# Sample attention of a hybrid decoder step: cached keys turned by VectorE in 32x32 blocks, four pages to a tile, and the delta rule's steps set between key tiles

## The chip, the cores and the metric

The kernel runs on one core of a Trainium2 chip. The metric is the device time of one launch in microseconds; three runs of the kernel before gave 927.4, 928.0 and 933.94 us, so its median is 928.0. The profiled execution took 927.22 us, of which 925.6 lie between its first and last instruction (its span).

## What is computed

One step of a small hybrid decoder for 256 prompt tokens and for 8 sequences of 4 new tokens (288 token columns in all), in fp32: a SwiGLU layer, a mixing layer and a second SwiGLU layer, each with adaptive norms. The change lies in the mixing layer, whose two head groups work on the same projection:

```python
go, s_new = gated_delta_rule(gq, gk, gv, g_log, beta, s0)
mo = attend(mq, mk, mv)
out = jnp.concatenate([go, mo], axis=-1) @ w_out

def moba_sample(q, k, v, cache_k, cache_v, page_table):
    k_full = cache_k[page_table[:, : j * ppb]].reshape(b, j, MOBA_BLOCK, h, hd)
    kmean = jnp.mean(k_full.astype(jnp.float32), axis=2)
    gate = jnp.einsum("bqhd,bnhd->bqhn", q.astype(jnp.float32), kmean)
    _, idx = lax.top_k(gate, n_sel)
    l_sel = selected_logits(q, k_sel, t, idx, slopes)
    return attend_merged(l_sel, v_sel, l_own, v_own)
```

The delta rule has 4 heads of width 128 (9 problems of 128 tokens here), the attention 8 heads of 64. Each of the 8 sequences has 2048 past keys in 8 blocks, of which every row selects 3. The logits are q . k less a penalty in proportion to the distance, and the softmax joins the selected blocks with the own new keys. The prompt attends to its own 256 tokens only. Since any block may be selected by some row, the kernel reads all 128 key pages and all 128 value pages of the cache (128 keys x 512 numbers, 256 KB each, 67 MB together).

## The kernel before

**The order of the whole.** Everything before the mixing layer's attention (up to about 400 us) and everything from the output projection `w_out` on (664 us) is the same code in both kernels, but for small pieces. Each engine has one instruction stream, written out by hand; semaphores tie them. What is told below is the stretch between, from 402 to 664 us.

**The key phase (402 to 530 us).** The 8 sequences go in two groups of four (`g`), and each group through 8 blocks of 256 keys (`blk`): 16 steps `n`. A step loads eight pages (one block of four sequences), on two queues: SP's takes the even pages and POOL's the odd ones (`page`, L533 and L534: a page number is read into a register, then 256 KB are issued). Keys land with the key index on the partitions, but q . k needs the head dimension there. So for each of the four 128-wide chunks `c` of a step (`m` = 4n + c) PE transposes eight 128x128 tiles into two PSUM banks (`T`, L704), ACT copies one bank to `ktb` (L1465), DVE the other (L1855), and PE multiplies with the queries `Qbd`, four sequences side by side in 32-column strips of the array (`logits`, L1015). `block_logits` on DVE (L1795 to L1798) adds up each block for its gate, adds the distance penalty and takes the maximum. Between, at chunk 2 of steps 0 to 9, stand the prompt's attention (`attention` on PE, `normalise` and `biased` on DVE, two exponentials and a copy on ACT, one head a step) and, in steps 9 to 12, the sums of squares for the delta rule's q and k.

**The value phase (530 to 664 us).** The delta rule of the first head group is a chain of small steps on 9 problems of 128x128 (groups `g` of 4, 4 and 1): decay rows, transposed k and v, Gram products, then 7 levels `l` that build the inverse of a triangular matrix. A level is: `level_mask`, products `P` (L1187), a copy with scale on DVE (L1971), products `XP` and `PX` (L1196, L1200), and four to six subtractions on DVE (L1985, L1986). The products rotate over five PSUM banks, and `s_ge` counts the copies out. Between these steps stand 16 steps `values(n)`: PE transposes a block's probabilities (ACT's exponentials, L1278), DVE copies them (L1847), and PE multiplies with 8 value pages (L1055). V pages have room for four half-steps in `kv`. `selection(g)` picks blocks for 128 rows once a group is complete. At 540.8 us ACT issues the four loads of the delta states (L1515). SP loads `w_out` into `kv` as the last value steps free it, before the delta rule is through.

**The end.** DVE sets `s_gdn` when the delta rule's output is in `mix`; PE then starts the 128 products with `w_out` (L1251).

Of the kernel before, what the change touches and what calls it, by code (L numbers as in the profile page):

```python
# [51 lines left out]
KU = 12  # L52
PHASE = NB * NBLK
# [6 lines left out]
def const_layout():  # L60

    names = [("ident", P), ("ones", P), ("tri", P), ("later", P), ("triS", P), ("laterS", P),
             ("lev", 7 * P), ("mh8", P), ("lower8", 64), ("biasS", PAST), ("biasO", 64),
             ("dist", 3 * P), ("hmask", 512), ("selbt", 16), ("bdm", NB)]
    at, out = 0, {}
    for n, w in names:
        out[n] = (at, at + w)
        at += w
    return out, at


def make_consts():
# [20 lines left out]
    put("mh8", (i[:, None] % 4 == i[None, :] // NS) & (i[:, None] < 8))  # L93
    n, m = np.arange(64) // 8, np.arange(64) % 8
    put("lower8", np.broadcast_to(m < n, (P, 64)))
    h, t = (i % 32) // NT, i % NT
    slope = 2.0 ** -(h + 1.0)
    put("biasS", slope[:, None] * (np.arange(PAST)[None, :] - PAST - t[:, None]))
    own = np.zeros((P, 2, 32))
    for g in range(2):  # L100
        j = np.arange(32)
        ok = (j[None, :] // NT == 4 * g + i[:, None] // 32) & (j[None, :] % NT <= t[:, None])
        own[:, g, :] = np.where(ok, slope[:, None] * (j[None, :] % NT - t[:, None]), NEG)
    put("biasO", own.reshape(P, -1))
# [4 lines left out]
    put("hmask", h[:, None] == np.arange(512)[None, :] // HD)  # L109
    put("selbt", (i[:, None] // 32) * NT + t[:, None] == np.arange(16)[None, :])  # L110
# [4 lines left out]
def build_program(nc, a, o):  # L115
    lay, cwidth = const_layout()
    with ExitStack() as ctx:
# [57 lines left out]
        eps = sb("eps", [P, 1])  # L175
# [14 lines left out]
        ptab = sb("ptab", [1, 2 * PHASE], I32)  # L190
# [33 lines left out]
        gE = shaped(sgf, 2, P)  # L224
# [16 lines left out]
        RS = shaped(region[:, mq_at:mq_at + 8 * TOK], 8, TOK)  # L241
# [10 lines left out]
        dead = const[:, lay["biasS"][0]:lay["biasS"][1]]  # L252
        st = [shaped(region[:, mq_at + NB * P * x:mq_at + NB * P * (x + 1)], NB, P) for x in range(3)]
        st.append(shaped(dead[:, NB * P:2 * NB * P], NB, P))
# [12 lines left out]
        at_ = carver(region)  # L267
        S = at_(2, PAST)
        ktb = shaped(wflat[:, 8964:8964 + 2048], 2, 2, 512)
        extra = wring[:, 3]  # L270
        pT = shaped(dead[:, 0:512], 2, 2, P)
        Om = dead[:, 512:1024]
        pex = shaped(sgf, 2, BLK)
        Qbd = shaped(adaf, 4, NB, 32)
        gts = at_(2, NBLK)
        bmx = at_(2, NBLK + 1)
        pen = at_(2, NBLK + 1)
        cmpA = at_(64)
        cmpB = at_(64)
        cnt = at_(NBLK)  # L280
        negm = at_(2)
        sown = at_(2, 32)
        pown = at_(2, 32)
        rsum = at_(2, NBLK + 1)
        rin = at_(8)
        ownT = at_(2, P)
# [81 lines left out]
        s_ge = sem("s_delta_copied")  # L368
# [20 lines left out]
        s_bmx = sem("s_block_max")  # L389
        s_qz = sem("s_qbd_zero")  # L390
        s_qbd = sem("s_qbd_ready")
        s_kv = [[sem(f"s_kv{i}_page{y}_landed") for i in range(KU)] for y in range(2)]
        s_vq = [[sem(f"s_vquad{i}_half{y}_landed") for i in range(4)] for y in range(2)]
# [4 lines left out]
        s_kt = sem("s_kt_psum")  # L398
        s_ktA = sem("s_kt_copied_act")
        s_ktD = sem("s_kt_copied_dve")  # L400
        s_qk = sem("s_logits_psum")
        s_lev = sem("s_logits_copied")
        s_pen = sem("s_selection")
        s_po = sem("s_own_probs")
        s_pe = sem("s_sel_probs")
        s_PT = sem("s_sel_probsT_psum")
        s_oT = sem("s_own_probsT_psum")
        s_pTs = sem("s_sel_probsT_copied")
# [82 lines left out]
        def v_quad(q):  # L491
            return (q + 2) % 4
# [1560 lines left out]
```

## Time and profile before

| | us |
|---|---|
| median of three runs | 928.0 |
| profiled execution | 927.22 |
| its span | 925.6 |
| PE busy (share of the span) | 859.5 (93%) |
| DVE busy | 501.3 (54%) |
| ACT busy | 304.6 (33%) |
| POOL busy | 113.9 (12%) |
| 16 DMA queues' engines: mean rate over the span | 221 GB/s |

All times are read from one profiled execution, in microseconds from the start of its span. "Busy" counts the time in which an engine works on a recorded instruction. An fp32 matmul appears as two records, so "x8" in a row of PE stands for four products. An instruction's duration includes its start-up, and the next one on the same engine begins some 0.1 us before it is over; where operations follow each other, the difference of their starts is the cost. The clock column gives the granted clock of TensorE, 1.00 for 2.4 GHz and 0.50 for 1.2 GHz.

### The profile page before, as it was taken

Reading aid. Unit: us, or ns where it says so; the run is one execution under the profiler, and the core shown is the slowest. Engines: PE = TensorE matmul, PEld = TensorE weight load, DVE = VectorE, ACT = ScalarE, POOL = GpSimd, SP = SyncE. Lnnn points to the kernel's source line nnn. Section 1 sums busy time; section 2 is a strip of 40 time slices with the busy share of each in tenths; the row PEclk is TensorE's granted clock in tenths of the full one; section 3 lists DMA queues with packets and bytes.
Section 4 is the critical chain, followed back from the end, with each engine's and each line's share of the span. In section 5 each row is a group of like instructions: output and inputs, shape, how many; then the busy total and the mean of one; then the engine's idle time right before and its main releaser. Section 6 shows DMA issues by size and latency. Waiting matters only on the chain.

```text
span 925.6 us, 19660 instructions
## 1 busy us (share of the span) xinstructions
PE 859.5 (93%) x7464; PEld 751.7 (81%) x7464; DVE 501.3 (54%) x961; ACT 304.6 (33%) x499; POOL 113.9 (12%) x197
## 2 busy tenths in 40 slices
PE   4889999999999999999999848998899999999996
PEld 3789999998997999966656524665777999999996
DVE  1445454543355667566656566657446565544363
ACT  1333333332323336453434511000225334432331
POOL 2000000000021000132223223230130000000021
PEclk9999999999999999999999988999999999999999
DMA  9999979785755252378778698898391555434401
GB/s 323 370 307 357 308 255 312 253 320 185 300 199 182 92 182 59 125 243 268 230 232 289 205 369 289 296 333 311 87 338 57 167 182 176 145 137 156 159 1 51
DMA packets 122163, 204.83 MB, mean 221 GB/s; under 512 B 7548, under 2 KB 56982, under 8 KB 121970
## 3 DMA queue, kind: packets, MB, share of 16 engines
q1 hardware_dynamic: 104976, 163.08, 50.9%
q0 software_dynamic: 11648, 38.45, 12.4%
q10 hardware_dynamic: 5474, 2.39, 1.0%
q8 instruction: 46, 0.75, 0.3%
q14 instruction: 19, 0.16, 0.1%
HBM read 199.01 MB, written 4.88 MB: 220 GB/s over the span
## 4 chain that ended last, share of the span: by engine, by line
PE 83%; DVE 5%; DMA 4%; issue 2%; ACTq 2%; ACT 2%; POOL 1%; POOLq 1%; DVEq 0%; SPq 0%
PE bank L741 19%; PE bank L743 18%; PE bank L742 18%; PE bank L704 8%; PE bank L1015 3%; PE bank L1251 3%; PE bank L723 3%; PE bank L1055 2%; DMA kv<-in_cache_v 2%; ACTq L1515 2%; DMA wring<-in_w_ada 1%; DMA region<-in_x_sample 1%; DVE wring_rounded L1590 1%; PE bank L1200 1%; PE bank L1187 1%
## 5 line engine op out<-in xcount | busy, mean ns | idle before, releaser
L741 PE MATMUL bank<-hn_rounded,kv_rounded 128*128 128x288 f32 x928 | 276.7, 298 | 5.9 <-DVE wring_rounded L1590 4.1
L742 PE MATMUL bank<-xs_rounded,kv_rounded 128*128 128x288 f32 x928 | 274.4, 296 | 0.0
L743 PE MATMUL bank<-hn_rounded,wring_rounded 128*128 128x288 f32 x928 | 273.6, 295 | 0.0
L1590 DVE TENSOR_TENSOR wring_rounded<-wring,kv_rounded 128x1024 fp32r<-128x1024 f32 (+1 forms) x164 | 188.3, 1198 | 71.7 <-ACT kv_rounded L1311 71.6
L1311 ACT CAST kv_rounded<-wring 128x1024 fp32r<-128x1024 f32 (+1 forms) x164 | 158.5, 1026 | 162.0 <-PE bank L743 109.7
L741 PEld LDWEIGHTS bank<-hn_rounded,kv_rounded 128*128 128x128 f32 x928 | 174.4, 188 | 10.2 <-DVE wring_rounded L1590 4.7
L743 PEld LDWEIGHTS bank<-hn_rounded,wring_rounded 128*128 128x128 f32 x928 | 175.4, 189 | 0.0
L742 PEld LDWEIGHTS bank<-xs_rounded,kv_rounded 128*128 128x128 f32 x928 | 174.9, 189 | 0.0
L741 PE MATMUL bank<-region_rounded,kv_rounded 128*128 128x288 f32 x352 | 105.5, 300 | 1.6 <-DVE modT L1582 1.6
L742 PE MATMUL bank<-region_rounded,kv_rounded 128*128 128x288 f32 x352 | 104.6, 297 | 0.0
L743 PE MATMUL bank<-region_rounded,wring_rounded 128*128 128x288 f32 x352 | 104.2, 296 | 0.0
L1644 DVE TENSOR_TENSOR sgate<-sgate,bank 128x288 f32<-128x288 f32 x44 | 20.0, 454 | 131.1 <-PE bank L743 123.2
L741 PEld LDWEIGHTS bank<-region_rounded,kv_rounded 128*128 128x128 f32 x352 | 66.6, 189 | 2.4 <-DVE modT L1582 2.0
L743 PEld LDWEIGHTS bank<-region_rounded,wring_rounded 128*128 128x128 f32 x352 | 67.0, 190 | 0.0
L742 PEld LDWEIGHTS bank<-region_rounded,kv_rounded 128*128 128x128 f32 x352 | 66.8, 190 | 0.0
L1855 DVE COPY wring<-bank 128x512 f32<-128x512 f32 x64 | 44.1, 689 | 41.7 <-PE bank L704 40.7
L1465 ACT COPY wring<-bank 128x512 f32<-128x512 f32 x64 | 37.3, 584 | 70.4 <-PE bank L704 70.4
L1278 ACT ACTIVATE sgate<-bank 128x288 f32<-128x288 f32 x44 | 18.1, 412 | 104.5 <-PE bank L743 104.5
L704 PEld LDWEIGHTS bank<-const,kv 128*128 128x128 f32 x352 | 37.7, 141 | 17.3 <-ACT wring L1465 12.4
L704 PE MATMUL bank<-const,kv 128*128 128x128 f32 x352 | 47.9, 279 | 0.0
L641 POOL TENSOR_TENSOR xs<-h 128x288 f32<-128x288 f32 x21 | 14.0, 668 | 255.3 <-DVE h L1668 254.9
L534 POOL DMA_DIRECT2D kv<-in_cache_v x64 | 34.4, 537 | 84.5 <-issue 54.0
(275 smaller groups left out, 987.4 us busy)
## 6 DMA issues: line engine op xcount, KB each, us to landing
wring<-in_ffn_up SPq DMA_DIRECT2D x44, 1024.0 KB, 7.7
wring<-in_w_ada SPq DMA_DIRECT2D x36, 1024.0 KB, 10.9
wring<-in_ffn_down SPq DMA_DIRECT2D x16, 1024.0 KB, 7.3
kv<-in_cache_v SPq DMA_DIRECT2D x64, 256.0 KB, 4.9
kv<-in_cache_v POOLq DMA_DIRECT2D x64, 256.0 KB, 5.2
wring<-in_w_in SPq DMA_DIRECT2D x14, 1024.0 KB, 6.4
kv<-in_cache_k SPq DMA_DIRECT2D x44, 256.0 KB, 4.5
kv<-in_cache_k POOLq DMA_DIRECT2D x44, 256.0 KB, 4.8
```

The lines of the kernel that those rows point to most:

```text
L534: eng.dma_start(dst, cache[which][bass.ds(p, 1), :, :].rearrange("a p n -> (a p) n")).then_inc(landed, 16)
L704: return nc.tensor.transpose(out, in_, ident[0:n, 0:n])
L723: m = nc.tensor.matmul(out[32 * g:32 * g + 32, 0:P], cT[:, k, :], wring[:, slot, k, g * P:(g + 1) * P], start=(k == 0), stop=(k == KD - 1) ...
L741: nc.tensor.matmul(out, hi, rhs_hi, start=start, stop=False)
L742: nc.tensor.matmul(out, hi, rhs_lo, start=False, stop=False)
L743: return nc.tensor.matmul(out, lo, rhs_hi, start=False, stop=stop)
L1015: ins = mm(ps[4][32 * b4:32 * b4 + 32, 0:BLK], Qbd[:, c, 4 * (n // NBLK) + b4, :], ktb[:, c % 2, b4 // 2, (b4 % 2) * BLK:(b4 % 2 + 1) * BL ...
L1251: m = mm(ps[4 * (1 - g) + i][:, 0:TOK], wo[g][:, k, i * P:(i + 1) * P], mix[:, k, :], start=(k == 4), stop=(k == 3))
L1311: nc.scalar.copy(whiR[:, u % 2, c, :], wring[:, n % RING, c, :]).then_inc(s_whi, 1)
L1465: nc.scalar.copy(ktb[:, m % 2, 0, :], ps[2 * (m % 2)][:, :]).then_inc(s_ktA, 1)
L1590: v.tensor_tensor(wringR[:, slot, c, :], wring[:, slot, c, :], whiR[:, u % 2, c, :], ALU.subtract).then_inc(s_wlo, 1)
L1855: v.tensor_copy(ktb[:, m % 2, 1, :], ps[2 * (m % 2) + 1][:, :]).then_inc(s_ktD, 1)
```

## The change

**Key tiles.** A unit is now a quad: four consecutive pages of one sequence, 1 MB in one tile of 128x2048 (`quad(n)`, 32 for the keys and 32 for the values, `NQ` = 4 per sequence). DVE turns the keys in place, `v.transpose` on 32x32 blocks (`keys_turned`). After it partition 32i + d holds number d of a 32-number slice for keys 32i to 32i + 31. The queries are spread to match (`query_weights` on POOL, from 16 small products on PE), and PE forms the logits straight from the turned quad, 16 products of 128 columns (L1104 after). The 512 PE transposes, and the copies L1855 and L1465, are gone.

**Rows.** A row of the logits is now (head, key quarter, token) of one sequence, with 512 columns. ACT copies the logits out in 8 pieces of 64 columns with their sums (`logits_out`), POOL adds the penalty, DVE takes the maxima (`block_max`), and the selection works on four sequences at once, with gates and sums added over key quarters by one product each (`gates`, `sums`). The exponentials are 9 instructions a sequence (`exponentials`). Probabilities reach the layout for the values by 64 products of 32 columns each per sequence with a 0/1 matrix (`transposed`, L1135 after).

**Loads.** SP alone issues the pages; POOL's queue issues none. Eight quads are loaded ahead during the input projection, then a quad is issued once the fourth before it has been used (`consumed(n - 4)`), so four are in flight at most. `w_out` goes to `wring`, which the delta rule uses, and is issued after the last value quad and `s_gdn`.

**Order.** A list of 85 portions (`K` a key quad, `G` a selection, `X` exponentials, `T` a turn of probabilities, `R` sums, `V` a value quad, `O` the last result) is cut to 34 points by `turns`. Points 0 to 9 lie in the prompt's attention and hold key quads 0 to 15; points 10 to 32 lie in the delta rule and hold 53 portions, to value quad 18; point 33 holds the other 16, after the delta rule.

**Other engines.** ACT takes over from DVE 19 of the delta rule's copies (`BY_ACT`; counters `s_geA` and `s_geD`), POOL takes the level masks, the decay masks, `QD` and the spread of `VN`. The first tile of the second SwiGLU no longer waits for `w_out` to leave `kv`.

The core of the diff:

```diff
-        def page(eng, table, dst, which, landed):
-            p = eng.value_load(ptab[0:1, bass.ds(table, 1)], min_val=0, max_val=NPHYS - 1)
-            eng.dma_start(dst, cache[which][bass.ds(p, 1), :, :].rearrange("a p n -> (a p) n")).then_inc(landed, 16)
+            for n in range(2 * QUADS):
+                if n < 8 and n % 2 == 0:
+                    sp.wait_ge(*released(("in", (3, 4, 5, 6)[n // 2])))
+                elif n >= 8:
+                    sp.wait_ge(*consumed(n - 4))
+                load_quad(n)
+            sp.wait_ge(s_gdn, 1)
+            for g in range(2):
+                for k in range(2):
+                    sp.dma_start(wo[g][:, 4 * k:4 * k + 4, :], wout[:, 4 * k:4 * k + 4, 512 * g:512 * g + 512]).then_inc(s_wo[g], 16)
...
+        def turns(point):
+            def upto(i):
+                return (0, 2, 4, 5, 7, 8, 10, 11, 13, 14, 16)[i] if i <= 10 else 16 + (len(PORTIONS) - 32) * (i - 10) // 23
...
+            def logits(b, q):
+                n = NQ * b + q
+                pe.wait_ge(s_X, n + 1)
...
+                for j in range(4):
+                    for c in range(4):
+                        m = mm(ps[5 + 2 * (b % 2)][32 * c:32 * c + 32, P * q:P * q + P], W[b % 2][:, j // 2, 2 * c + j % 2, :],
+                               keys[:, :, 4 * c + j, :], start=(j == 0), stop=(j == 3), tile_position=(0, 32 * c))
...
+                for x in range(4 * NQ):
+                    for kb in range(4):
+                        m = mm(ps[5][32 * kb:32 * kb + 32, 32 * x:32 * x + 32], row[:, 32 * x:32 * x + 32], cst("pick")[:, 32 * kb:32 * kb + 32],
+                               start=True, stop=True, tile_position=(0, 32 * kb))
...
+            def keys_turned(n):
+                dve.wait_ge(*quad_landed(n))
+                v.transpose(quad(n), quad(n)).then_inc(s_X, 1)
...
-            for m in range(4 * 2 * NBLK):
-                dve.wait_ge(s_kt, 2 * m + 2)
-                dve.wait_ge(s_qk, m + 1)
-                v.tensor_copy(ktb[:, m % 2, 1, :], ps[2 * (m % 2) + 1][:, :]).then_inc(s_ktD, 1)
+            for s in range(HM + 2):
+                normalise(s)
+                biased(s)
...
+                attend(s)
```

**Where it moves instructions.** First DVE at level 1 of the delta rule. Before, between the two blocks of operations stand a mask pass and a copy of probabilities:

```order
L1971 TENSOR_TENSOR wring<-bank,region 128x512 x2
L1971 TENSOR_TENSOR wring<-bank,region 128x128
L1933 TENSOR_TENSOR wring<-wring,const 128x512 x2
L1843 COPY region<-bank 32x128
L1847 COPY const<-bank 128x256
L1985 TENSOR_TENSOR wring<-wring,bank 128x512
L1986 TENSOR_TENSOR wring<-wring,bank 128x512
```

The same place in the changed kernel (L2093 is the scaled copy, L2104 and L2105 are the subtractions, L1943 a turn of a key quad):

```order
L1943 STREAM_TRANSPOSE kv<-kv 128x2048
L1948 TENSOR_REDUCE region<-region 128x8
L1943 STREAM_TRANSPOSE kv<-kv 128x2048
L2093 TENSOR_TENSOR wring<-bank,region 128x512 x2
L2093 TENSOR_TENSOR wring<-bank,region 128x128
L1980 TENSOR_REDUCE cst<-bank 128x4
L1981 RECIPROCAL cst<-cst 128x4
L1983 TENSOR_TENSOR cT<-bank,const 32x128
L1943 STREAM_TRANSPOSE kv<-kv 128x2048
L2104 TENSOR_TENSOR wring<-wring,bank 128x512
L2105 TENSOR_TENSOR wring<-wring,bank 128x512
```

One to three key turns now stand in front of every step of the chain on DVE. On PE, in the program of before, the same level has the value products between `P` and `XP`:

```order
L1187 MATMUL bank<-wring 128x128 x9
L704 MATMUL bank<-const,region 32x128
L704 MATMUL bank<-const,sgate 128x128 x2
L1055 MATMUL bank<-kv,const 32x512 x8
L1061 MATMUL bank<-region 32x512 x4
L1196 MATMUL bank<-wring 128x128 x4
L1200 MATMUL bank<-wring 128x128 x4
```

In the changed kernel's program of PE (L1288 is `P`, L780 and L1123 are the own probabilities and the sums, L1104 the logits of a turned quad, L1296 and L1300 are `XP` and `PX`):

```order
L1288 MATMUL bank<-wring 128x128 x9
L780 MATMUL bank<-const,cst 32x128
L1123 MATMUL bank<-cst,const 128x36
L1104 MATMUL bank<-kv,adasb 32x128 x16
L1296 MATMUL bank<-wring 128x128 x4
L1300 MATMUL bank<-wring 128x128 x4
```

PE comes to `XP` only behind logits that wait for DVE's turns. From point 20 on value quads (16 products of 8 x 128 each) stand there, and at eight points the 64 small products of `transposed`.

## Rows read from the trace of the kernel before

**Rows 1.** Page, section 4: shares of the chain by line
```profile
PE bank L741 19%; PE bank L743 18%; PE bank L742 18%; PE bank L704 8%; PE bank L1015 3%; PE bank L1251 3%; PE bank L723 3%; PE bank L1055 2%; DMA kv<-in_cache_v 2%; ACTq L1515 2%; DMA wring<-in_w_ada 1%; DMA region<-in_x_sample 1%; DVE wring_rounded L1590 1%; PE bank L1200 1%; PE bank L1187 1%
```
**Rows 2.** By windows: busy us (xinstructions) per engine, clock, DMA share, GB/s
```profile
402.00:530.00 128.00, 123.04 (x1127) 77.78 (x1125) 82.66 (x186) 58.26 (x127) 31.20 (x58) 1.00 0.73 240
530.00:664.00 134.00, 108.38 (x924) 72.16 (x923) 83.54 (x199) 13.19 (x35) 33.10 (x61) 0.94 0.81 282
664.00:696.00 32.00, 31.28 (x128) 24.24 (x128) 14.22 (x29) 8.78 (x8) 12.36 (x16) 1.00 1.04 321
```
**Rows 3.** By windows: line L704 alone (transposes on PE)
```profile
402.00:530.00 128.00, 73.21 (x530) 56.41 (x528) 1.00 0.73 240
```
**Rows 4.** Groups by form, 400 to 664 us (count, busy us, mean ns)
```profile
L1855 DVE COPY wring<-bank 128x512 f32<-128x512 f32 x64 | 44.1, 689 | 41.7 <-PE bank L704 40.7
...
L1465 ACT COPY wring<-bank 128x512 f32<-128x512 f32 x64 | 37.3, 584 | 70.4 <-PE bank L704 70.4
```
**Rows 5.** Timeline of PE (start us, us, what): own logits, a key step
```profile
399.35 1.49 PE L972 MATMUL bank<-region,adasb 128*32 128x32 f32 x64 [1.90 <-DVE wring L1759]
...
446.88 0.64 PE L1015 MATMUL bank<-wring,adasb 128*32 128x256 f32 x8
447.45 1.09 PE L704 MATMUL bank<-const,kv 128*128 128x128 f32 x8
```
**Rows 6.** Timeline of DVE: one step of the prompt's attention
```profile
405.24 0.56 DVE L1780 SCALAR_TENSOR_TENSOR wring<-const,bank 128x384 f32<-128x384 f32 x1 [0.16 <-PE bank L984]
...
406.04 0.41 DVE L1784 TENSOR_REDUCE wring<-wring 128x1 f32<-128x256 f32 x1
...
410.94 0.29 DVE L1771 TENSOR_SCALAR wring<-wring 128x128 f32<-128x128 f32 x1
411.14 0.34 DVE L1772 TENSOR_SCALAR wring<-wring 128x256 f32<-128x256 f32 x1
```
**Rows 7.** Timeline of DVE: wide operations in SBUF
```profile
527.34 1.34 DVE L1873 COPY wring<-region 128x1152 f32<-128x1152 f32 x1
...
547.20 1.22 DVE L1919 TENSOR_TENSOR wring<-wring,const 128x1024 f32<-128x1024 f32 x1
```
**Rows 8.** Timeline of ACT and its queue: states issued, a probability
```profile
540.82 11.50 ACTq L1515 DMA_DIRECT2D region<-in_state_gdn  x3
552.36 3.44 ACTq L1515 DMA_DIRECT2D const<-in_state_gdn  x1
...
557.34 0.51 ACT L1278 ACTIVATE sgate<-region 128x256 f32<-128x256 f32 x1 [0.35 <-PE bank L704]
```
**Rows 9.** Timeline of PE: values and products of one level
```profile
611.19 1.92 PE L1055 MATMUL bank<-kv,const 128*32 128x512 f32 x16
613.04 1.16 PE L1196 MATMUL bank<-wring 128*128 128x128 f32 x8
614.04 1.06 PE L1200 MATMUL bank<-wring 128*128 128x128 f32 x8
```
**Rows 10.** Chain in order of time (start us, us, what)
```profile
605.43 3.63 PE bank L1161 x128
...
664.48 31.29 PE bank L1251 x128
```
**Rows 11.** By windows: after a wait of PE, and the value stream
```profile
576.00:578.00 2.00, 1.11 (x8) 0.19 (x8) 0.08 (x1) 0.00 (x0) 0.78 (x2) 0.82 1.00 393
578.00:580.00 2.00, 2.00 (x11) 1.60 (x8) 0.00 (x0) 0.00 (x0) 0.83 (x2) 0.50 1.04 402
...
630.00:640.00 10.00, 10.00 (x79) 5.74 (x72) 8.12 (x25) 0.00 (x0) 0.00 (x0) 1.00 1.03 371
```
**Rows 12.** Timeline of SP's queue: value pages issued in pairs
```profile
521.05 1.43 SPq L534 DMA_DIRECT2D kv<-in_cache_v  x2
...
523.25 1.42 SPq L534 DMA_DIRECT2D kv<-in_cache_v  x2
```
**Rows 13.** Groups by form of POOL over the span
```profile
L644 POOL TENSOR_TENSOR xs<-xs 128x288 f32<-128x288 f32 x18 | 15.3, 853 | 1.4
```

More of the change, by code:

```diff
@@ L552, in stream_rest @@
[L552 to L567 removed]
+        AB_TURN = 20
@@ L662, in _ @@
+            for point in range(29, POINTS + 1):
+                attend(point)
             pool.wait_ge(*copied(("S2",)))
@@ new lines, in attend @@
+            def attend(point):
+                for what, b, *q in turns(point):
+                    if what == "K":
+                        logits(b, q[0])
+                    elif what == "G":
+                        gates(b)
+                    elif what == "R":
+                        sums(b)
+                    elif what == "T":
+                        transposed(b)
+                    elif what == "V":
+                        values(b, q[0])
+                    elif what == "O":
+                        gathered(b)
@@ L1095, in bank @@
+            for s in range(HM + 2):
+                attention(s)
+                if s < 8:
+                    qk_sum(s)
+                attend(s)
             def bank(step):
@@ L1432, in _ @@
                 zqkv(q)
+            act.wait_ge(s_q4, 1)
+            nc.scalar.copy(sgf[:, 0:512], ps[6][:, :]).then_inc(s_q4e, 1)
             for q in range(0, 6, 2):
@@ new lines, in probs_transposed, with attend @@
+            def probs_transposed(b):
+                act.wait_ge(s_PT, b + 1)
+                if b >= 2:
+                    act.wait_ge(s_PV, NQ * (b - 1))
+                nc.scalar.copy(PT[b % 2], ps[5][:, :].rearrange("p (x n) -> p x n", x=4 * NQ)).then_inc(s_PTe, 1)
+            def attend(point):
+                for what, b, *q in turns(point):
+                    if what == "K" and q[0] == NQ - 1:
+                        logits_out(b)
+                    elif what == "X":
+                        exponentials(b)
+                    elif what == "T":
+                        probs_transposed(b)
@@ L1485, in _ @@
+            act.wait_ge(s_cg, 1)
+            act.wait_ge(s_csil, CC)
+            for s in range(HM + 2):
+                if s < 8:
+                    fn((RSq if s < 4 else RSk)[:, s % 4, :], Cv[:, s, :], ACT.Square).then_inc(s_qks, 1)
                 if 1 <= s <= HM:
@@ new lines, in _ @@
+            act.wait_ge(*copied(("cum",)))
+            fn(ecum, cum, ACT.Exp).then_inc(s_ecum, 1)
+            attend(10)
+            act.wait_ge(s_okv, 96)
+            for j in range(3):
+                b = filled(("row", j))
+                fn(sel(EG, j), grp3(b, j), ACT.Exp).then_inc(s_eg, 1)
+                nc.scalar.copy(sel(gR, j), grp3(b, j)).then_inc(s_geA, 1)
+            attend(11)
+            act.wait_ge(s_df, 1)
+            fn(DT, DT, ACT.Exp).then_inc(s_dt, 1)
+            act.wait_ge(s_bek, 1)
@@ L1518, in _ @@
+            nc.scalar.copy(goT[:, :, P:SEQ], grp3(filled(("o1",)), 0)).then_inc(s_geA, 1)
             act.wait_ge(*copied(("o1",)))
             fn(sqg[:, 0:HG, :], goT, ACT.Square).then_inc(s_go, 1)
+            attend(32)
+            for hh in range(HG):
+                fn(sqg[:, HG + hh, :], filled(("rms", hh))[:, 0:TOK], ACT.Ln, scale=1.0 / P, bias=eps[:, 0:1]).then_inc(s_geA, 1)
             act.wait_ge(*copied(("rms", HG - 1)))
-            own(fn(sqg[:, HG:8, :], sqg[:, HG:8, :], ACT.Ln))
```

889 lines of the change are left out of this document (456 added, 433 removed).

## Prediction

> **What bounds the kernel now.** I read the shares of the chain first. The three split products of the dense layers (L741 to L743) hold 55% of the span, and the change does not touch them; of the attention's lines L704, the transposes on PE, holds 8%, L1015 3% and L1055 2% [rows 1]. The view by windows then gives the stage in two pieces. From 402 to 530 us PE is busy for 123 of 128 us: PE is the bound, and L704 alone is busy for 73.2 of it [rows 2, 3]. From 530 to 664 us PE is busy for 108 of 134 us at a mean clock of 0.94, and the DMA engines for 81% of the time: a chain of short steps, filled with value products, near to the limit of the transfers [rows 2]. After it come the products with `w_out`, 31.3 us from 664.5 [rows 10]. What I forecast is when these start in the changed kernel; everything outside 402 to 664.5 us I take as unchanged.
>
> **What goes.** A chunk of a key step costs PE 0.57 us of logits and 1.02 us of transposes (446.88 to 447.45, and the 1.6 us rhythm) [rows 5]; 64 chunks are the 102 us that fill the first piece. 64 copies on DVE (44.1 us) and 64 on ACT (37.3 us) go too [rows 4].
>
> **What comes, piece by piece.** A *key turn* (DVE, 128x2048, 32 of them) is seen nowhere in this trace. From the widest one-element-a-cycle operations, 1.34 us at 1152 and 1.22 us at 1024 columns, an element costs about 1 ns [rows 7]; so 1.34 + 896 x 0.00102 = 2.25 us, 2.2 in a row. Bounds: the scalings L1771 and L1772 grow by 0.05 us for 128 more columns [rows 6], which would give 1.1 us; two passes would be 4.4 us. I take 2.2, since a turn, like the copy of rows 7, has one source and no scalar, and no row shows such an operation faster. The Trainium skill (Vector Engine (DVE) Microarchitecture Reference, section 3.8) says that the transposing array sustains one element per cycle per lane; no run here shows it yet, and the sum by it would be the same.
>
> *Logits of a quad*: 16 products of 128 columns in four strips. L1161's 128 records, 64 products of this shape, take 3.63 us [rows 10], so 0.9 us. *Values of a quad*: the same count and width, 0.9 us; before, four pages cost as much (1.85 us from start to start for eight, L1055) [rows 9]. *Turn of a sequence's probabilities*: 64 products of 32 columns; the own logits took 1.49 us for 64 records, that is 32 products [rows 5], so 3.0 us, eight times. *ACT's pieces of 64 columns*: 0.51 us for 256 columns [rows 8]; with 0.1 us less from the next one's early start and 192 columns less, 0.35 us each, 2.8 us for the 8 of `logits_out` and 3.2 for the 9 of `exponentials`. *POOL*: 0.85 us at 288 columns [rows 13], some 1.2 us at 512.
>
> *First ten points.* DVE carries them: 16 turns (35 us); eight steps of the prompt's attention at about 1.8 us (L1780 0.56, two maxima of up to 0.41, scalings of 0.29 and 0.34, a reciprocal) [rows 6], 14 us; copies out, block maxima and the spread of the decays, 5 us; waits for PE and ACT, 8 us. Sum 62 us: 402 to 464. Loads don't hold it: 8 quads are there, and a quad takes 1.049 MB / 371 GB/s = 2.83 us [rows 11].
>
> *Points 10 to 20.* ACT first ends quad 15's logits and two exponentials (5 us), then issues the delta states. That cost its queue 11.5 + 3.4 us, next to saturated loads [rows 8]; here fewer pages are in flight, so I take 10 (bounds 4 and 15). Behind it on ACT stand the exponential of `cum` and the decay rows' copies (3 us), and DVE waits for the last of them: it goes on at 482. Then DVE has 14 turns (31 us) and about 25 us of the chain and a selection, all in order. PE's products no longer overlap with that: `XP` stands behind logits, these behind the turn. A group of four products takes 0.9 us (613.04 to 614.04 to 614.93) [rows 9], and a level has two to seven such groups; counted through to level 2 and with 0.9 us of logits ahead of each exchange, this leaves 23 us in which DVE waits. Sum 79 us: the keys end at 554, value quad 0 is used at 561. In this piece 16 quads and the states need 51 us of transfer, in 97: the queue runs dry.
>
> *Points 21 to 32.* Before, level 3 to the end of the delta rule took from about 618 to 664, of it 13 us of value steps and a wait for a page, so 33 us. New beside it: 18 value quads 16 us, four turns of probabilities 12, the second selection 3.6, the sequences' products L1161 3.6 [rows 10], and exponentials on ACT between two copies of the chain 3.2. Sum 72 (rounded): 561 to 633. Transfers would need 43 us for these 15 quads, and the portions don't ask for them sooner.
>
> *Point 33 and `w_out`.* Quads 20 to 31 are then fetched at the rate of the transfers: 12 x 2.83 = 34 us. The delta states' output (2.36 MB, POOL's queue) falls in the same time: 6.4 us. The first half of `w_out`, once loaded under the value steps, now follows the last quad: 2.1 MB, 5.7 us, with 3 us of issue and landing. Sum 49: the products start at 682, against 664.5. SP keeps up: a page took it 1.1 us [rows 12], of which most is the read of its number, now one read for four pages, so about 2.5 us for a quad of 2.83.
>
> **Sum.** 927.2 + 17.5 for the later start + 1.5, since PE comes to `w_out` out of a time with 0.9 us of work in 2.8, where the clock may be at half. To this 3 us for slow products on the path: after a wait of 2.4 us the clock fell to 0.82 and 0.50 [rows 11], and products take twice as long there. That is 949 us, against the profiled 927.2 and the median of 928.0. Nothing of the gain is left: the 102 us of PE work were replaced by DVE work and by waits in order, and 13 value quads are left over at the end, with nothing beside them.
>
> **Rivals.** *Transfers set the pace* (faster, the other side). If DVE's 23 us of waiting in points 10 to 20 are hidden to 8, and the states' issue costs 6, the value part begins at 542; if it then runs at the rate of the transfers throughout, 28 quads (79 us), 6.4, 5.7 and 3 give 636, and the kernel takes 927.2 - 28 + 1.5 = about 900. For it: DVE and PE are both busy for little over half of the new stage; the queue never had four whole megabytes in flight before. Against it: three engines follow one order of portions. It decides where the products start before 655.
>
> *Gain and loss cancel*, within 9 us of 928: the chain of the forecast with its waits 12 to 25 us shorter.
>
> *Half clock throughout.* With some 0.9 us of products between turns, PE is busy for about half of the stage. If the clock stays at 0.50 in it, the delta rule's products (53 us in 0.9 us groups) take twice as long; about 35 us of that lie on the chain, and the wait for transfers hides 8 of them: 949 + 27 = 976. Against it: at 0.94 with gaps before [rows 2], it recovered each time. The Trainium skill (TensorE: Matmul & The Clock Gate, section on HAM oscillation) says that a kernel whose products come in bursts shorter than its waits for data starts each burst cold. The trace agrees for single waits; no row shows it for a whole stage.
>
> *A turn costs two passes.* 32 x 2.2 = 70 us more, nearly all on DVE's path: about 1010.
>
> **Chances.** Transfers set the pace, or something between that and a gain of 1%: 0.30, faster. Cancelled: 0.16. The forecast 0.30, half clock 0.18, two passes 0.05, and 0.01 for what I don't see, all slower: 0.54. A measurement of this kernel can tell about 1% from no change, 9.3 us; the three classes are cut there. The forecast's own range is 938 to 962. The range that holds 8 in 10 takes in the first and the fourth case: 900 to 985. It leaves out the two passes and the tails of those two.
>
> **What would show it.** A turn of 2.2 us in the groups by form; key quad 15 turned near 464; DVE waiting 10 us or more for ACT behind the state loads; the last turn near 554; DMA share under 0.7 until 630 and near 1 after; the first product of `w_out` at 682, released by the load of `w_out`. Wrong by a lot if a turn is not 2.2 us, if the clock column reads 0.5 through the delta rule, or if the share of the DMA engines is near 1 from 480 on.

## The result: 989.4 us in place of 929.4

Four runs of the changed kernel gave 983.9 to 991.4 us, median 989.4; four of the kernel before, taken beside them, 927.4 to 933.9, median 929.4. The ratio is 1.063 (95% interval 1.057 to 1.069). The forecast was 949, with a range of 900 to 985: the sign was right, the size a third of what was measured (21 us against 60).

The profiled execution took 983.9 us (the shortest of the four), 981.8 of them its span. The page's chain, as [rows 1] showed it for before:

```profile
## 4 chain that ended last, share of the span: by engine, by line
PE 48%; DVE 12%; SPq 5%; issue 3%; DMA 1%; ACT 1%; ACTq 0%; DVEq 0%
PE bank L817 10%; PE bank L819 10%; PE bank L818 10%; DVE kv L1943 5%; PE bank L1356 3%; PE bank L1104 3%; SPq L630 3%; PE bank L1288 2%; SPq L626 2%; PE bank L780 1%; PE bank L1164 1%; PE bank L1300 1%; DMA wring<-in_w_out 1%; DVE wring L1943 1%; PE bank L1296 1%
```

The turns (L1943) and the logits behind them (L1104) are now on the chain, and so is SP's own queue (L630 issues a page, L626 reads page numbers), which [rows 1] does not list. The windows of the changed stage, in the form of [rows 2] (busy us of PE, weight loads, DVE, ACT, POOL; granted clock, DMA share, GB/s):

```profile
402.00:480.00 78.00, 56.64 (x656) 36.11 (x646) 54.71 (x75) 23.67 (x120) 7.85 (x13) 0.74 0.48 158
480.00:580.00 100.00, 54.91 (x801) 45.77 (x805) 65.94 (x79) 28.24 (x151) 26.53 (x25) 0.74 0.58 185
580.00:642.00 62.00, 55.81 (x1349) 47.62 (x1339) 32.99 (x81) 17.24 (x95) 13.33 (x10) 1.00 0.73 238
642.00:718.00 76.00, 48.79 (x1114) 34.40 (x1113) 7.15 (x20) 8.70 (x16) 4.39 (x5) 0.68 0.88 294
```

Nothing is saturated in the first two. The last turn ends at 579.3 and the first value product runs at 585.2. At 642 the chain passes to SP's queue. PE comes to point 33, with its 13 value quads, at 660.8 (the end of L1341, the delta rule's last products), and the products of `w_out` start at 717.8 against 664.5 [rows 10]. That is 53.3 of the 56.2 us between the two spans; the rest of the kernel takes 264.0 in place of 261.1 us.

**The key portions: a circle of waits.** The chain of waits of the changed kernel, in order of time (start us, us, what), around two portions, and then what DVE did next (from its own timeline, with its idle time in brackets):

```profile
427.65 2.22 DVE kv L1943
429.87 0.57 DVE region L1948
430.44 2.23 DVE kv L1943
432.71 1.94 PE bank L1104 x32
434.64 0.72 PE bank L1066 x2
435.37 0.85 PE bank L1067 x2
```

```profile
436.26 0.56 DVE L1930 SCALAR_TENSOR_TENSOR wring<-const,bank 128x384 f32<-128x384 f32 x1 [2.97 <-PE bank L1067]
```

DVE turns a quad while PE stands still; PE then does that quad's logits, and only behind them the next head's scores (L1067), for which DVE stands still for 2.97 us. Each engine works while the other waits. What DVE waited for from 402 to 580 (us in total, times, longest), 55.6 us with the rows left out:

```profile
DVE wring L1930 <- PE bank L1067: 16.2, 8, 3.0
DVE wring L2093 <- PE bank L1288: 12.8, 6, 4.0
DVE wring L2056 <- ACT wring L1634: 4.6, 1, 4.6
DVE wring L2063 <- PE bank L780: 4.4, 1, 4.4
...
DVE wring L2048 <- ACT xs L1383: 2.8, 1, 2.8
```

A clock of 0.74 over both windows makes each of PE's shares in that circle longer: a quad's logits took 1.08 us at full clock (446.03) and 1.94 at half (432.71).

**The end: SP's queue.** The chain from 676 on, one quad of SP (L626: page numbers, L630: the four issues), and its end:

```profile
676.01 0.30 SPq L626
...
677.51 0.33 SPq L630
678.03 0.33 SPq L630
678.55 0.33 SPq L630
679.06 0.33 SPq L630
679.45 0.30 SPq L626
...
707.56 10.07 DMA wring<-in_w_out
717.76 2.26 PE bank L1356 x4
```

A quad takes SP 3.44 us (676.01 to 679.45): 1.5 for its page numbers, 1.94 for four issues 0.52 apart. The transfers could do it in 2.83 [rows 11]. Before, SP and POOL each issued half of the pages. With some stalls on top, the loads of the last 16 value quads (16 to 31; quads 16 to 18 belong to point 32) took from 643 to 707, 4.0 us each. Until 660.8 PE still has the delta rule's work beside them; from there to 718 it waits 23.6 us for value pages.

### The profile page after: what moved, and what is told of

Its sections match the earlier page's. It is cut to its first block, busy times and chain, and to the rows that moved or that the text cites. A ratio compares the mean times of both kernels' runs of the same rounds, so it can differ in the third digit from the quotient of the medians.

```text
span 981.8 us, 22701 instructions
## 1 busy us (share of the span) xinstructions
PE 845.9 (86%) x9312; PEld 765.8 (78%) x9312; DVE 492.2 (50%) x830; ACT 309.0 (31%) x715; POOL 94.3 (10%) x118
## 4 chain that ended last, share of the span: by engine, by line
PE 48%; DVE 12%; SPq 5%; issue 3%; DMA 1%; ACT 1%; ACTq 0%; DVEq 0%
PE bank L817 10%; PE bank L819 10%; PE bank L818 10%; DVE kv L1943 5%; PE bank L1356 3%; PE bank L1104 3%; SPq L630 3%; PE bank L1288 2%; SPq L626 2%; PE bank L780 1%; PE bank L1164 1%; PE bank L1300 1%; DMA wring<-in_w_out 1%; DVE wring L1943 1%; PE bank L1296 1%
## 5 line engine op out<-in xcount | busy, mean ns | idle before, releaser
L1104 PE MATMUL bank<-kv,adasb 128*32 128x128 f32 x896 | 44.9, 364 | 59.9 <-DVE kv L1943 59.9
L1104 PEld LDWEIGHTS bank<-kv,adasb 128*32 128x32 f32 x896 | 32.5, 145 | 71.4 <-DVE kv L1943 69.3
L1943 DVE STREAM_TRANSPOSE kv<-kv 128x2048 f32<-128x2048 f32 x28 | 63.4, 2290 | 0.0
L1383 ACT ACTIVATE sgate<-bank 128x288 f32<-128x288 f32 x44 | 18.1, 411 | 104.2 <-PE bank L819 104.2
L799 PE MATMUL bank<-wring,cT 128*32 128x128 f32 x1152 | 37.1, 284 | 7.3 <-DMA wring<-in_w_ada 7.3
L799 PEld LDWEIGHTS bank<-wring,cT 128*32 128x32 f32 x1152 | 32.4, 114 | 10.3 <-issue 9.8
```

What stands on the lines that cost most here:

```text
L799: m = nc.tensor.matmul(out[32 * g:32 * g + 32, 0:P], cT[:, k, :], wring[:, slot, k, g * P:(g + 1) * P], start=(k == 0), stop=(k == KD - 1) ...
L1104: m = mm(ps[5 + 2 * (b % 2)][32 * c:32 * c + 32, P * q:P * q + P], W[b % 2][:, j // 2, 2 * c + j % 2, :], keys[:, :, 4 * c + j, :], start= ...
L1943: v.transpose(quad(n), quad(n)).then_inc(s_X, 1)
```

## The experiments

All are edits of the changed kernel, three timing rounds each. The ratio is to the kernel before in the same rounds. Its median there was 928.6 to 931.8, so differences between medians of different runs, as the text gives them, are good to some 3 us. The last two columns come from the profiled execution: the end of the last key turn and the start of `w_out`'s products.

| run | median us | ratio, 95% interval | last turn | w_out |
|---|---|---|---|---|
| changed kernel | 989.4 | 1.063 (1.057 to 1.069) | 579.3 | 717.8 |
| e1_even | 971.9 | 1.049 (1.043 to 1.054) | 564.4 | 707.1 |
| e2_fixed_pages | 977.2 | 1.051 (1.046 to 1.056) | 581.2 | 711.5 |
| e3_wout_early | 987.6 | 1.065 (1.061 to 1.070) | 582.6 | 718.8 |
| e4_two_queues | 981.0 | 1.057 (1.051 to 1.062) | 583.5 | 714.0 |
| e5_even_two_queues | 966.2 | 1.040 (1.034 to 1.047) | 567.5 | 699.6 |
| e6_spare_products | 981.3 | 1.054 (1.048 to 1.059) | 573.3 | 717.9 |
| e7_small_turns | 931.6 | 1.003 (0.999 to 1.006) | 526.7 | 664.9 |
| e8_all_three | 958.4 | 1.031 (1.026 to 1.037) | 560.4 | 692.8 |
| e9_late_logits | 957.1 | 1.029 (1.025 to 1.033) | 551.4 | 689.8 |
| e10_late_logits_all | 940.1 | 1.011 (1.007 to 1.014) | 546.0 | 675.0 |
| e11_late_logits_spare | 950.0 | 1.022 (1.015 to 1.029) | 555.6 | 686.4 |
| e12_no_late_logits | 963.0 | 1.033 (1.029 to 1.038) | 568.8 | 700.3 |
| e13_first_values_later | 942.5 | 1.013 (1.006 to 1.020) | 545.8 | 677.4 |
| e14_small_turns_all | 921.6 | 0.990 (0.987 to 0.993) | 522.6 | 656.5 |

### The end: who sets its pace?

Theory: SP's queue. Rival: the transfers, whose engines are busy for 0.88 of that stretch.

```diff
-    ... 16 + (len(PORTIONS) - 32) * (i - 10) // 23
+    ... 16 + (len(PORTIONS) - 16) * (i - 10) // 23
```

> The portions behind point 9 are dealt out three to a point, so that none is left for point 33 (before: two or three to a point up to point 32 and 16 at the end). Changed kernel: last key quad turned at 579.3 us, first value quad used at 584.9, 16 value quads from 641.4 to 714 with PE and DVE nearly idle, w_out's products from 717.8. Theory 'order': the end is long because the table leaves 16 portions with nothing beside them, and the keys are long because DVE waits 36 us for links of the chain (482 to 579) that the table spreads over 21 points. Then the keys end 10 to 15 us earlier (a third fewer waits in them), 12 of the 16 late quads are fetched beside the delta rule, whose stretch grows by their products (0.9 to 1.9 us each, 10 to 20 us), and the products of w_out start 25 to 40 us earlier: about 955 us against 989. Rival 'transfers or SP's queue': the late quads cost their 4.0 us each wherever they stand, w_out starts at most 10 us earlier: 980 to 989.

The expectation counts 16 late value quads; by the table point 33 holds 13, and PE is busy with points 29 to 32 from 641.4 to 660.8. The edit took 17.5 us off, between theory and rival: the keys end 15 us earlier, as the theory said, but `w_out` starts only 10.7 us earlier, not 25 to 40. The value quads now stand beside the delta rule and hold it up (its last products start at 691.4 in place of 658.6): 26.5% of the chain from 560 to 710 is L630 and 13.2% L626. The order alone does not help an end that the queue paces.

```diff
+    fixed = n >= QUADS + 16      # these quads: constant page numbers, nothing read
```

> Value quads 16 to 31 are fetched from pages whose numbers are constants in place of the ones that SP reads from the page table (other pages, so other numbers in the output; same bytes, same packets). In the changed kernel SP needs 3.4 us for a quad even when nothing holds it (1.3 us for four reads of page numbers, 4 x 0.52 for the transfers), and these 16 quads take 64 us (643 to 707), 4.0 us each. Theory 'SP's queue sets the pace': without the reads a quad costs SP 2.1 us, the transfers' 2.83 us take over, and 16 quads need about 16 x 2.9 = 46 us and something for the outputs (6.4): w_out starts 10 to 15 us earlier, 975 to 980 us. Rival 'transfers set the pace' (share of the DMA engines 0.88 between 642 and 718): nothing changes, within 3 us of 989, and the rate stays at about 294 GB/s.

12.2 us less in the median, the theory's number. In the profiled execution `w_out` starts 6.3 us earlier: point 33 takes 44.3 us (from 667.2) in place of 57.0 (from 660.8), but begins later. The transfers of the same stretch, changed kernel (642 to 718), then this one (642 to 712):

```profile
DMA packets 11385, 22.31 MB, mean 294 GB/s; under 512 B 1146, under 2 KB 1146, under 8 KB 11372
```

```profile
DMA packets 12908, 25.10 MB, mean 359 GB/s; under 512 B 1309, under 2 KB 1309, under 8 KB 12896
```

The same engines move the same kind of packets 22% faster when SP has less to do. So a mean share of 0.88 was not saturation; here it is 1.00.

```diff
+    elif what == "V" and 16 <= NQ * b + q[0] < QUADS - 4:     # on ACT
+        w = NQ * b + q[0] + 4
+        act.wait_ge(*consumed(QUADS + w - 4))
+        ... two page numbers, two act.dma_start into quad(QUADS + w)
```

> Of value quads 20 to 31 two of the four pages are read and asked for by ACT, whose queue has next to nothing then; SP does the other two. Theory 'SP's queue sets the pace': these 12 quads no longer cost SP 3.4 to 4 us each but 1.8, the transfers' 2.83 take over, and w_out starts 9 to 14 us earlier (975 to 980 us). Rival 'transfers set the pace': within 3 us of 989. A third outcome is possible: ACT's reads and waits stand in its order in front of the last exponentials, which would show as PE waiting for ACT.

8.4 us less in the median, a little under the theory's 9 to 14, though the intervals of the two ratios overlap. The rate is clearer, 347 GB/s in place of 294 (share 0.98), and point 33 takes 47.6 us in place of 57.0: the theory again. The Trainium skill (DMA: Bandwidth & Descriptors, section Rules for kernel authors) says that spreading transfers over the issuing engines brings no bandwidth and saves only the issuing engine's time. The trace agrees with the reason and shows where it matters: SP's time was the bound, so the saved time was bandwidth.

```diff
+    if n == 2 * QUADS - 4:
+        sp.wait_ge(s_gdn, 1)     # and issue wo[0] here, ahead of the last four quads
```

> The first half of w_out is asked for ahead of the last four value quads in place of behind them; everything else stands. In the changed kernel it is asked for at 707.1 and lands 10.1 us later, all of it on the chain. Theory 'SP's queue sets the pace': its two issues cost SP under 1 us, its 2.1 MB fill the engines while SP reads page numbers, and w_out starts 6 to 9 us earlier (about 981 us). Rival 'transfers set the pace': the bytes only change places, the last quads come 5.7 us later, and no more than the latency of about 3 us is gained (986 or more).

Nothing (`w_out` starts at 718.8, the median falls by 1.8 us, inside the spread). The rival had this one. The chain shows why (us, us, what): the last value quad now lands later, and what followed it had been waiting for exactly that.

```profile
710.97 5.21 DMA kv<-in_cache_v
716.22 1.06 PE bank L1167 x32
717.28 0.37 PE bank L1173 x8
717.68 0.36 DVE cst L2000
718.09 0.41 PE bank L1151 x2
718.75 1.39 PE bank L1359 x3
```

> Both of the edits that helped: three portions to a point (as in the first run), and two pages of every value quad from 4 on are read and asked for by ACT (as for quads 20 to 31 in the run with two queues). In the run with three portions to a point the chain of waits from 580 to 698 us is SP's own queue, 3.4 us and more for each of 31 value quads. Theory 'SP's queue sets the pace': with half of the issues taken off, the transfers' 2.83 us a quad come to bind; 28 quads, the outputs' 6.4 and w_out's 5.7 + 3 us from about 562 end near 660 to 675 in place of 707, 925 to 945 us. Rival 'the order binds': PE waits for links of the delta rule between the value quads whatever the queue does, and w_out starts at 695 or later, 960 us or more.

966.2, what its rival said: SP's issues are gone from the larger pieces of the chain, and PE's products in their written order have taken their place (from 555 to 705 the values' are 20.7% of it, the delta rule's 22%); `w_out` starts at 699.6. SP had been the first bound of the end, the order was the second, close behind it.

### The key portions: turns, clock, or order?

> Only the first 32 of 2048 columns of each key quad are turned (about 0.2 us in place of 2.30), so the logits are computed from keys that are not turned; everything else stands. It takes 67 us of DVE's work out of the key portions. Theory 'DVE's turns carry the key portions' (what the prediction's first two pieces say): the keys end 45 to 60 us earlier (near 525 in place of 579), and about 930 to 945 us in all, less if the queue of loads then binds. Rival 'the links of the chain and the loads carry them': DVE then waits for PE, ACT or for a key quad to land (SP 3.4 us a quad), the keys end near 550, 960 us or more.

This kernel leaves out nearly all of each turn, so its logits are wrong and only its time counts. 57.8 us less for 67 us of DVE work taken away: in this order almost the whole of a turn is on the chain. That confirms the frame of the forecast's first two pieces (DVE carries the keys). DVE's idle time does not fill the gap: it waits 60 us for PE, ACT and POOL in the shorter stretch (402 to 530) and 10 for keys, so the links of the chain are long by themselves.

```diff
+    for _ in range(6):
+        mm(ps[5 + 2 * (b % 2)][:, P * q:P * q + P], ident, tri, start=True, stop=True)
     pe.wait_ge(s_X, n + 1)
```

> The changed kernel with 6 products of 128 columns of constants ahead of the wait for each key turn (192 in all, 1.35 us a time at full clock, into the columns that the logits then start anew), so that PE has work while DVE turns. In the changed kernel the granted clock is 0.66 to 0.83 in the key portions, where PE was never below 0.9 before. Theory 'half clock costs much': the clock goes back to 0.95 and more between 402 and 580; a group of four delta products takes 0.9 in place of up to 1.7, logits 1.1 in place of 1.9, DVE's waits shrink by 15 to 20 us, and the keys end near 562: about 972 us. Rival 'the clock costs little': the products that it slows lie beside DVE's turns or wait for it; the spare ones cost what they give back, within 4 us of 989. Third: they stand in the way (6 at half clock are 2.7 us, more than a turn) and it gets slower by up to 20 us.

The clock did what the theory said, in the first window fully, in the second partly:

```profile
402.00:480.00 78.00, 67.58 (x876) 53.66 (x871) 57.03 (x76) 25.84 (x121) 12.35 (x17) 0.96 0.56 175
480.00:580.00 100.00, 73.19 (x1111) 65.67 (x1114) 66.71 (x83) 27.84 (x164) 24.66 (x25) 0.87 0.59 185
```

The gain is half of what it said: 8.1 us in the medians, with intervals that just touch. In the profiled execution the keys end 6.0 us earlier, but `w_out` starts at the same time (717.9). The same products in e8 against e5, in the same rounds, are clearer: 958.4 (957.3 to 963.1) against 966.2 (963.8 to 974.4).

> Three portions to a point, two queues for value quads from 4 on, and the 6 spare products before each wait for a turn. Theory 'half clock costs much': 10 to 17 us below the run without the spare products. Rival: no difference beyond 4 us, or slower, since with three portions to a point PE has more of its own work between the waits.

So slow products cost about 8 us net of the spare ones; the clock is a cause, not the main one.

```diff
     def attend(point):                       # on PE; the same on ACT for logits_out
+        for b, q in late:
+            logits(b, q)
+        late.clear()
         for what, b, *q in turns(point):
             if what == "K":
-                logits(b, q[0])
+                late.append((b, q[0]))
```

> The changed kernel with one edit: PE takes the logits of the keys turned at a point only at the next point, behind that point's own products, and ACT copies a row's logits out one point later too. So PE no longer stands in wait for a turn in front of the products that DVE waits for next. In the changed kernel DVE's idle time before L1930 is 16.2 us (402 to 480), before the exchange's operations and other links of the chain 36 us (482 to 579), most of it with PE's products queued behind logits, these behind the turn. Theory 'waits in order': at least half of those 52 us go, the keys end 25 to 35 us earlier (545 to 555 in place of 579), and the total falls to 955 to 965, unless SP's queue (3.4 us a quad) takes some of it back. Rival 'the waits are the chain's own': DVE waits for PE's products at half clock with or without the logits ahead; within 5 us of 989.

32.3 us less, as the theory said; the keys end 27.9 us earlier and `w_out` starts 28.0 earlier. What DVE waited for from 402 to 552 is 29.1 us in all, against 55.6 (402 to 580):

```profile
DVE wring L1940 <- PE bank L1067: 8.9, 4, 3.9
DVE kv L1953 <- DMA kv<-in_cache_k: 8.3, 5, 2.5
DVE region L1958 <- POOL region L704: 4.3, 1, 4.3
DVE wring L2103 <- PE bank L1293: 3.5, 4, 1.1
...
```

26.5 us of waiting gone, 28 us of time gone. Cut at the ends of the 16th and of the last turn, the windows of this kernel are

```profile
402.00:478.60 76.60, 50.64 (x656) 34.06 (x656) 56.01 (x81) 23.96 (x105) 9.57 (x15) 0.74 0.51 163
478.60:551.40 72.80, 50.59 (x778) 44.27 (x779) 62.85 (x80) 27.60 (x164) 25.04 (x25) 0.78 0.71 234
```

where the changed kernel needed 103 us for the second (476.3 to 579.3), at a clock of 0.74. The clock hardly rose, so the rival, that the waits are those of slow products, falls. No operation was removed or made cheaper: the logits, which nobody awaits soon, no longer stand in front of products that DVE awaits at once. The edit also moves ACT's copies of the logits a point later. Of the 26.5 us, 7.4 were waits for ACT (L1634 and L1383), and the two moves were not tried apart. But the gain lies behind the states alone. In points 0 to 9 the 16th turn ended at 478.6 (476.3 before the edit): of the 16.2 us before L1930 8.9 stayed, and 4.3 for POOL and 3.4 for key quads (from 402 to 472) came in their place. What would shorten these ten points was not found.

### Together, and what is left

> Late logits, two queues for value quads from 4 on, the portions dealt out so that 8 in place of 16 are left for point 33, and the first half of w_out asked for ahead of the last four quads. No spare products. From the run with three to a point and two queues (966) the late logits take what they take in the run alone (theory 'waits in order': 25 to 35 us), and the w_out load's 9 us on the chain shrink to 3 or less: 930 to 940 us. If the late logits give nothing: 958 to 965.

940.1: these four edits together give 49 of the 60 us back. `w_out`'s load is off the chain here, the last value quads' transfers and products are on it.

> The kernel before in this list with 4 spare products of 128 columns ahead of each quad's logits. If half clock still costs there, 4 to 8 us less than without them; if the late logits keep PE busy by themselves, the same or up to 10 us more (32 x 0.9 us of PE time).

9.8 us slower, though the clock rises from 0.77 to 0.94 in the second half of the keys (from 475): once PE has its own work beside the turns, the spare products cost more than they give back.

> The run with all three edits (958 us: three to a point, two queues, 6 spare products) with 8 portions left for point 33 in place of none and the first half of w_out asked for ahead of the last four value quads; no late logits. There w_out's products wait 9 us for their load, behind the square sums, the gate and the product with z (7 us) that all stand behind the last value quad. Theory: with value quads still to come behind these, both hide: w_out starts 8 to 14 us earlier, 945 to 950 us. Rival: what PE has to do before w_out stays the same and the transfers of the last quads come later: within 4 us of 958.

Its theory falls: 963.0 against 958.4 for the run without these two edits. `w_out`'s load no longer ends the chain, but a transfer of value pages (12.5 us from 679.5) does in its place, as in e3.

> The kernel with late logits, two queues, 8 portions left for point 33 and w_out asked for early (940 us), with its first two value quads one point later, behind the level's products that stood behind them (DVE waited 10.1 us for these at 547). Theory 'the value quads start in the wrong place': 5 to 9 us less, 931 to 935, level with the kernel before. Rival: the value quads' transfers bind from there to w_out anyway (28 x 2.83 us from 548), and the shift gives 2 us or less.

The rival again (942.5): from 530 to 680 PE waits 23.9 us for value pages, against 21.9 without the edit.

> The kernel with late logits, two queues, 8 portions left for point 33 and w_out asked for early (940 us), with only the first 32 of 2048 columns of each key quad turned (0.2 in place of 2.30 us), so that its logits come from keys that are not turned. In the changed kernel the same took 57.8 us off. Theory 'DVE is still the bound of the key portions': 35 to 55 us less (885 to 905). Rival 'with late logits the turns lie beside PE and the loads': key quads are waited for then (SP 3.4 us a quad, 22 quads from 427), and 10 to 25 us less (915 to 930).

18.5 us less, in the range of the rival; again the turns are left out, and the 921.6 are no time of a kernel that computes the right logits. With the logits late, two thirds of the turns' cost have gone beside other work. Without turns, DVE waits for keys in place of turning them (402 to 540):

```profile
DVE kv L1966 <- DMA kv<-in_cache_k: 43.2, 16, 5.8
DVE wring L2127 <- PE bank L1306: 13.4, 4, 11.2
```

So what keeps the best version 10 us above the kernel before is no single term that I took away. Keys still come through SP alone at 3.44 us a quad with four slots; splitting those issues as well was not tried, nor was a mix of keys turned by PE and by DVE. Whether either gets below 929 stays open.

## Why the prediction was wrong

The forecast put the start of `w_out` at 682; it was 717.8. By its own steps:

| step | forecast | measured | difference |
|---|---|---|---|
| points 0 to 9 (402 to the last of 16 turns) | 62 | 74 | +12 |
| ACT and the state loads, until DVE goes on | 18 | 6 | -12 |
| points 10 to 20, to the first value product | 79 | 103 | +24 |
| points 21 to 32, to the delta rule's last product (660.8) | 72 | 76 | +4 |
| point 33, to `w_out` | 49 | 57 | +8 |

**Single prices: mostly right.** A turn takes 2.21 us from one start to the next, and in the groups by form:

```profile
L1943 DVE STREAM_TRANSPOSE kv<-kv 128x2048 f32<-128x2048 f32 x28 | 63.4, 2290 | 0.0
```

The 2.2 of the forecast holds, 1.08 ns an element; the rival of two passes falls. POOL's 1.27 us at 512 columns (1.2), and values of a quad at 0.91 to 0.99 (0.9), at full clock, hold too; logits of a quad took 1.08 (0.9) at full clock. A sequence's turned probabilities were priced at 3.0 and took 1.23: a 32-column product with 32-column strips costs less than half of the row it was taken from [rows 5]. ACT's pieces were over-priced too (1.75 us for the eight of `logits_out`, 2.8 forecast). So points 21 to 32 come near their 72 in part by luck: four turns of probabilities cost 5 us and not 12, and other things took that back. The second selection took 5.7 us (596.4 to 602.1) in place of 3.6, and PE stood 4.4 us in the middle of two value quads' products, for a reason that the profile does not name.

**The states' issue: over-priced.** I took 10 us from [rows 8], where the loads were saturated; here ACT's queue was held for 5.1 in four pieces, side by side with other work, and about 1 us of it on the chain:

```profile
479.11 0.40 ACTq L1612 DMA_DIRECT2D region<-in_state_gdn  x1
479.54 0.86 ACTq L1612 DMA_DIRECT2D region<-in_state_gdn  x1
480.43 1.61 ACTq L1612 DMA_DIRECT2D region<-in_state_gdn  x1
482.07 2.20 ACTq L1612 DMA_DIRECT2D spare<-in_state_gdn  x1
```

This error hid the one before it: DVE went on at 482.3, as forecast (482), for the wrong reasons.

**The waits: the term that failed first.** I named the mechanism for points 10 to 20 (`XP` stands behind logits, these behind the turn) and priced the waits at 8 us before the states and 23 behind. It was 55.6, from 402 to 580, of which 22 lie before the states and 33 behind. Four things were missing. In points 0 to 9 I charged the circle hardly anything, though `biased` waits for scores that stand behind two quads' logits in just the same way (16.2 us at L1930). I priced PE's links at full clock and put the clock in as 3 us in one lump; at 0.74 each link in the circle was longer, worth about 8 us by e6 and e8. I counted 14 turns behind 482, there are 16 (4.4 us). And I let POOL's new work beside DVE cost nothing, where it cost 4.3 us behind 482 (last section). From 482 to the first value product the waits make +10 (33 in place of 23), the turns +4.4 and POOL +4.3 of the 24 us; the remaining 5 were not traced. That most of the waits behind the states are order, and go when the order does, is what e9 shows; for the 12 us of points 0 to 9 it shows only that the order of the logits alone is not their cause.

**SP's queue: the term that failed second.** "SP keeps up" with 2.5 us a quad came from [rows 12]: 1.1 a page, of which I took most to be the read of its number. It is the other way round: four reads cost 1.5, the four issues 1.94. 0.9 us a quad decide which side of the transfers' 2.83 it falls on, and I did not check that margin. Quads 20 to 31, the forecast's twelve, kept SP from 656.9 to 707.1, 4.2 us each, 50 us in place of 34. Part of that fell before point 33, and the delta states' output, which I had added as 6.4 us, ran beside it; so the step is only 8 us over its 49. With SP's work on these loads cut, the same step took 44.3 us (e2) and 47.6 (e4): the queue's part is 9 to 13 us.

**The rivals.** *Transfers set the pace* was wrong for the changed kernel (DMA share 0.48 and 0.58 until 580). *Half clock throughout* forecast 976, nearest to the result, but by a mechanism that was worth 8 us, not 27: the clock was at 0.74, not 0.50, and at 1.00 from 580 to 642. The result lies just beyond the range's end, because the range was built from one cause at a time, while waits and queue failed together.

**Signs set beforehand.** Right: the turn's 2.2 us; a DMA share under 0.7 until 580. Wrong: that share was 0.73 from 580 to 642 and 0.88 after, not under 0.7 until 630 and near 1 after; quad 15 turned at 476, not 464; DVE's wait for ACT behind the state loads was 2.8 us, not 10; the last turn at 579, not 554; `w_out` at 718, not 682, though released by its own load as said.

## What to carry to other kernels

When work moves to another engine, the time is in the circle it closes: list, for each instruction that a second engine awaits at once, what now stands ahead of it in its own engine's order, and let the work that nobody awaits soon trail by one step; here that alone (on PE and on ACT) was worth 32 us, more than half of the loss. When two issuing queues become one, compare the queue's time for a tile (all its register reads and issues) with the transfer's time for the same bytes before calling the transfers the bound.

## What was unexpected of the hardware

**POOL's work holds DVE up.** A product of the selection, 128x256 with both inputs in SBUF, took 2.45 us when POOL ran beside it; the same line took 0.43 in the second selection, where POOL was idle. DVE's timeline, then POOL's (start us, us):

```profile
498.75 0.43 DVE L1963 TENSOR_TENSOR region<-region,const 128x256 f32<-128x256 f32 x1
499.21 2.45 DVE L1964 TENSOR_TENSOR region<-region 128x256 f32<-128x256 f32 x1
...
599.28 0.43 DVE L1964 TENSOR_TENSOR region<-region 128x256 f32<-128x256 f32 x1
```

```profile
499.02 2.35 POOL L730 TENSOR_TENSOR wring<-wring,const 128x1024 f32<-128x1024 f32 x1 [12.97 <-ACT wring L1383]
```

POOL's operation began 0.2 us earlier; DVE's ended 0.3 us behind POOL's end, as if it had only run then. The 1152-wide product at L2048 took 3.63 us beside two of POOL's (2.61 and 1.30 us from 482.07); in e9, where POOL was idle then, the same operation took 1.34:

```profile
478.57 1.34 DVE L2058 TENSOR_TENSOR wring<-region,xs 128x1152 f32<-128x1152 f32 x1
```
The Trainium skill (SBUF — State Buffer, section Who interferes with whom) says that a DVE instruction with two SBUF inputs contends with a GpSimd instruction that reads SBUF, and that of two engines on the shared ports the one that issues first holds them for its whole instruction, while the other blocks. The trace agrees: POOL began first, and DVE waited it out. The change had moved the masks and penalties to POOL; these two cases are 2.0 and 2.3 us on the chain, an effect that the forecast had at nothing.

**A mean busy share of 0.88 was no saturation here.** From 642 to 718 the DMA engines show 0.88 at 294 GB/s; with less work for SP 1.00 at 359. Even from 670 to 690, at a share of 0.91, the rate was 304.
